# Inverse roots of the latent ranks by a DRAM scratch and one broadcast load instead of two spreads by matmuls

## The reference, cut to what matters

```
def _rms_norm(x, g):
    y = x * lax.rsqrt(jnp.mean(x * x, axis=-1, keepdims=True) + RMS_EPS)
    return y * g

proj = h @ w_in
fq, fk, fv, fg, c_q, c_kv, k_r = jnp.split(proj, cuts, axis=-1)    # c_q: 384 wide, c_kv: 256 wide
fox_out = _fox_attention(fq, fk, fv, log_f)                         # 8 heads of 64
q  = (_rms_norm(c_q,  q_norm)  @ w_uq)                              # 8 heads of 64 + 32
kv = (_rms_norm(c_kv, kv_norm) @ w_ukv)                             # 8 heads of 64 + 64
mla_out = _mla_attention(q_nope, q_rope, k_nope, k_rope, v)
m = concatenate([fox_out, mla_out]) @ w_out
```

## Time and profile before

| | |
|---|---|
| median of 3 runs | 1998.29 us (1997.29 to 1999.68) |
| profiled execution | 1997.75 us |
| its span | 1996.0 us |
| mean granted TensorE clock | 0.998 |
| TensorE busy | 1964.0 us, 98% of the span |
| VectorE busy | 1169.2 us, 59% |
| ScalarE busy | 845.9 us, 42% |
| DMA | 167.66 MB, 84 GB/s |
| start of even_ukv (step 144) | 138.87 us from the start of the span |

### The profile page before, as it was taken

The page is one execution under the profiler, slowest core; times in us unless marked ns, Lnnn a source line. Parts: engine busy times, 40 slices in busy tenths (PEclk is TensorE's granted clock), DMA queues, the critical chain, the costliest instruction groups (busy, mean ns, idle before and its releaser), DMA issues.

```text
span 1996.0 us, 29508 instructions
## 1 busy us (share of the span) xinstructions
PE 1964.0 (98%) x11549; PEld 1616.6 (81%) x11549; DVE 1169.2 (59%) x1939; ACT 845.9 (42%) x1347; POOL 23.6 (1%) x28
## 2 busy tenths in 40 slices
PE   9999999999999999999999999999999899999998
PEld 7776798888888787898888888778778678888887
DVE  6556477534547766567533555877777656424532
ACT  5456544333335455454332333644664633212222
POOL 0111000000000000000000000000000000000000
PEclk9999999999999999999999999999999999999999
DMA  6222122222222111123223224111111122222221
GB/s 215 77 72 96 43 76 95 89 100 106 87 90 98 69 64 64 64 85 106 82 93 115 91 83 138 43 44 45 63 44 44 63 81 89 105 97 94 94 96 64
DMA packets 27583, 167.66 MB, mean 84 GB/s; under 512 B 3272, under 2 KB 3400, under 8 KB 11600
## 3 DMA queue, kind: packets, MB, share of 16 engines
q1 hardware_dynamic: 25872, 161.69, 23.0%
q10 hardware_dynamic: 1600, 4.42, 0.7%
HBM read 162.93 MB, written 2.11 MB: 83 GB/s over the span
## 4 chain that ended last, share of the span: by engine, by line
PE 85%; DVE 7%; ACT 5%; issue 2%; DMA 1%; SPq 0%; DVEq 0%; ACTq 0%
PE bank L506 24%; PE bank L508 24%; PE bank L507 23%; PE bank L1146 2%; PE bank L781 1%; ACT hH L1343 1%; ACT wH L1343 1%; DVE hL L2120 1%; PE bank L970 1%; PE bank L804 1%; PE bank L994 1%; DVE x L2116 1%; PE bank L793 1%; ACT L1343 1%; PE bank L1232 1%
## 5 line engine op out<-in xcount | busy, mean ns | idle before, releaser
L506 PE MATMUL bank<-hH,wH 128*128 128x512 f32 x1368 | 550.0, 402 | 2.0 <-DVE hL L2082 2.0
L508 PE MATMUL bank<-hH,wL 128*128 128x512 f32 x1368 | 532.9, 390 | 0.0
L507 PE MATMUL bank<-hL,wH 128*128 128x512 f32 x1368 | 531.9, 389 | 0.0
L1343 ACT ACTIVATE wH<-raw 128x2048 fp32r<-128x2048 f32 (+3 forms) x199 | 294.1, 1488 | 119.9 <-PE bank L508 105.1
L506 PEld LDWEIGHTS bank<-hH,wH 128*128 128x128 f32 x1368 | 257.4, 188 | 60.0 <-issue 7.1
L508 PEld LDWEIGHTS bank<-hH,wL 128*128 128x128 f32 x1368 | 257.2, 188 | 54.8
L507 PEld LDWEIGHTS bank<-hL,wH 128*128 128x128 f32 x1368 | 257.9, 189 | 46.4
L2031 DVE TENSOR_TENSOR wL<-raw,wH 128x2048 fp32r<-128x2048 f32 x96 | 219.7, 2288 | 125.6 <-ACT wH L1343 125.6
L506 PE MATMUL bank<-mH,wH 128*128 128x512 f32 (+1 forms) x610 | 232.8, 382 | 0.0
L507 PE MATMUL bank<-mL,wH 128*128 128x512 f32 (+1 forms) x610 | 232.6, 381 | 0.0
L508 PE MATMUL bank<-mH,wL 128*128 128x512 f32 (+1 forms) x610 | 232.6, 381 | 0.0
(11 more groups left out here) (344 smaller groups left out, 2864.4 us busy)
## 6 DMA issues: line engine op xcount, KB each, us to landing
raw<-in_ffn_up SPq DMA_DIRECT2D x44, 1024.0 KB, 4.8
raw<-in_mlp_up SPq DMA_DIRECT2D x16, 1024.0 KB, 4.8
raw<-in_mlp_down SPq DMA_DIRECT2D x16, 1024.0 KB, 4.8
raw<-in_ffn_down SPq DMA_DIRECT2D x16, 768.0 KB, 4.3
raw<-in_odd_in SPq DMA_DIRECT2D x12, 1024.0 KB, 4.8
raw<-in_dn_qkv SPq DMA_DIRECT2D x12, 1024.0 KB, 4.8
raw<-in_ffn_down SPq DMA_DIRECT2D x16, 640.0 KB, 3.8
raw<-in_even_in SPq DMA_DIRECT2D x7, 1024.0 KB, 4.9
```

The source lines that it names most:

```text
L506: mm(out, a, c, start=first, stop=False, skip_group_check=joined)
L507: mm(out, a, d, start=False, stop=False, skip_group_check=joined)
L508: return mm(out, b, c, start=False, stop=last, skip_group_check=joined)
L1343: return nc.scalar.activation(out, in_, func, **kw)
```

## The change

The inverses travel through a DRAM scratch of 8 x 128 floats. At step 121 ScalarE stores `stat[:, 48:56]` so that the DRAM holds them in the order of the tokens, c_q first and then c_kv: 128 partitions with 8 values each, written to 8 rows of 128 values. At step 125 ScalarE waits for that store and asks for one load that brings all 1024 values to each of the 128 partitions (`rank_inverse`, 128 x 1024 float32, in a region of SBUF that is free at that time). The two spreads leave TensorE's list. VectorE's scalings read rank_inverse instead of bank 7. The scaling of tiles 0 to 2 moves from step 124 to 132, of tiles 3 and 4 from 127 to 134; the lows from 126 to 134 and from 129 to 136; the highs from 125 to 133 and from 128 to 135.

```diff
+        rank_inverse = sb("rank_inverse", [P, 2, SEQ], F32, qF_at + 4 * 18 * SEQ)
...
                 if t == 116:
                     rank_sums()
-                if t == 123:
-                    pe.wait_ge(*at("cq.inverse"))
-                    spread_tokens(7, 48).then_inc(*tick("spread_pe", "cq.spread"))
-                if t == 127:
-                    pe.wait_ge(*at("cq.t2"))
-                    spread_tokens(7, 52).then_inc(*tick("spread_pe", "ckv.spread"))
...
-                if t in (125, 128):
-                    his("cq", range(3) if t == 125 else (3, 4), cqH, lambda k: cqRaw[:, k, :])
+                if t == 121:
+                    act.wait_ge(*at("cq.inverse"))
+                    act.dma_start(dram["rank_rows"].rearrange("c p -> p c"), stat[:, 48:56], allow_slow_non_contiguous=True)\
+                        .then_inc(*tick("rank_stored", "cq.stored", 16))
+                if t == 125:
+                    act.wait_ge(*at("cq.stored"))
+                    act.dma_start(rank_inverse[:].rearrange("p a n -> p (a n)"),
+                                  dram["rank_rows"].rearrange("c p -> (c p)").unsqueeze(0).to_broadcast([P, 2 * SEQ]))\
+                        .then_inc(*tick("rank_loaded", "cq.spread", 16))
+                if t in (133, 135):
+                    his("cq", range(3) if t == 133 else (3, 4), cqH, lambda k: cqRaw[:, k, :])
...
-                stt(cqRaw[:, k, :], cqRaw[:, k, :], g, bank[7][:], ALU.mult, ALU.mult).then_inc(*tick("norm_dve", f"cq.t{k}"))
+                stt(cqRaw[:, k, :], cqRaw[:, k, :], g, rank_inverse[:, int(k >= 3), :], ALU.mult, ALU.mult).then_inc(*tick("norm_dve", f"cq.t{k}"))
...
-                if t in (124, 127):
-                    dve.wait_ge(*at("cq.spread" if t == 124 else "ckv.spread"))
-                    for k in range(3) if t == 124 else (3, 4):
+                if t in (132, 134):
+                    dve.wait_ge(*at("cq.spread"))
+                    for k in range(3) if t == 132 else (3, 4):
                         rank_scaled(k)
-                if t in (126, 129):
-                    for k in range(3) if t == 126 else (3, 4):
+                if t in (134, 136):
+                    for k in range(3) if t == 134 else (3, 4):
                         lo_tile("cq", k, cqRaw[:, k, :], cqH, cqL)
...
+        dram["rank_rows"] = nc.dram_tensor("rank_rows", (8, P), F32, kind="Internal").ap()
```

## The result

The changed kernel takes 2003.9 us (median of 9 runs, 2003.09 to 2006.11) against 1998.72 us of the kernel before in the same session: ratio 1.0027, 95% interval 1.0018 to 1.0035. It is slower by more than the 0.2% that can be told from no change. The profiled execution has a span of 2002.1 us, 6.1 more than before. The forecast was 1996.5, range 1994.9 to 2001.0, with 0.13 for slower.

What follows compares the result with a forecast made beforehand. TensorE was taken to bound the kernel: 0 for the unchanged arithmetic, minus 1.78 us for the spreads, 0 for a hidden store and load, so minus 1.8 from the median 1998.29 gives 1996.5 us, range 1994.9 to 2001.0.

Steps and rivals of the forecast that it cites:

- What bounds the kernel, and what the removal is worth: TensorE, busy 98% of the span, bounds; removing two spreads of 0.89 us each from its path gives minus 1.78 us.
- S: Latency of ScalarE's store of the inverses to DRAM, taken as 4.0 us; up to 4.8 us costs TensorE nothing.
- the upper bound of 13.2: Store latency in us at 183 ns for each of 64 packets on an engine, read from the stored 2 KB rows.
- my lower bound: Store latency of 2.0 us: 64 packets per engine at 8.5 ns each, from the program's first load.
- The rival for "slower": Each 4-byte write takes its own DRAM time, from 142 ns a packet; TensorE stands at step 144; 2004.9 us; chance 0.12.
- The estimate of 2.7 us: Store latency by the skill page's figures: about 10.5 ns a packet and some 2.0 us fixed; the sum unchanged.
- The floor of 1.49 us: Least store latency: gate rows' store issued at 38.97, its waiting load at 40.46, so 1.49 us at most.
- The store's issue: ScalarE's store at step 121 goes out at 118.4, after its earlier work ends at 118.37.
- The three deadlines for the store: Landing by 123.2 for TensorE's step 144; by 124.0 for tile 11's turn and for the values at 127.9, called looser.
- the formula max(0, S - 4.8): TensorE's stall ahead of step 144: store latency beyond the 4.8 us from issue at 118.4 to deadline 123.2.
- The clock: A clock fall behind TensorE's wait at step 144 would add more; the trace's fall, 4 us at 0.57, lost 1.7 us.
- my chance of a third for missing it: Two rivals with TensorE waiting at step 144: part of the gain comes back, chance 0.22; slow store, chance 0.12.

Runs made afterwards that it cites:

- the turned store: Changed kernel plus one transposing matmul on TensorE and a ScalarE copy, so the store writes eight runs of 512 bytes: median 1997.07 us against 1999.05, ratio 0.9987.
- the one row: Changed kernel storing only one of the eight columns, 128 runs of 4 bytes side by side in 512 bytes; load reads the gate's rows: 1999.77 us, single run.

## Why the prediction was wrong

**What bounds the kernel, and what the removal is worth: right.** Minus 1.78 us was the term; the store of 32-byte runs gives 1.76, with nothing else changed. The wait for the rotated queries moved along (1.21 us at 170.74 in the changed kernel, 1.31 before). A stage shorter by the 1.8 us of the sum is what the changed kernel shows with a quick store.

**How long is S: the step that failed.** I took 4.0 us, and 12.44 was measured, near the upper bound of 13.2. That it stayed under the bound was luck: the bound was 183 ns a packet on the DMA engine, and the packets passed at 9 ns each, my lower bound, all of them in 0.8 us. I chose 4.0 by the wrong likeness: a 4-byte write was set beside a 32-byte read because of its size. The time lies behind the packets, and it depends on where the writes go: it is there when they are close neighbours in the DRAM (12.44 us) and gone when they are 64 bytes apart (4.94). The rival for "slower" came nearest, with a chance of 0.12: it named the neighbours in a 512-byte row. But it put the price on each 4-byte write, from 142 ns a packet on; 512 writes cost nearly as much as 1024, and 1024 writes that lie apart cost next to nothing. That the neighbours come from different partitions, as the rival had it, is neither shown nor refuted. Why close writes delay each other no run shows.

The Trainium skill ("DMA: Bandwidth & Descriptors", "Specifications") says that below 512 bytes the DMA reads, changes and writes back. The runs fit a stretch of 512 bytes and don't exclude 256. They add the price, some 45 ns for each further write into 512 bytes, and that small writes apart from each other have next to none. The estimate of 2.7 us from that page's figures was further off than mine, and its 2.0 us fixed is the page's figure for DMAs that GpSimd issues, not for ScalarE's.

**The floor of 1.49 us: right for a quiet DMA, not here.** The store of the gate rows was made with the DMA engines idle (its 16 packets are all that the earlier trace rows has). Here some 3 us pass behind the weights of unit 10, which SyncE had asked for 0.57 us earlier:

```profile
115.98 0.33 SPq L439 DMA_DIRECT2D raw<-in_even_uq  x1
```

I never put the two side by side, though SyncE's request stands in the trace of the kernel before.

**The store's issue: 118.4 in the text, 116.55 in the trace.** ScalarE's queue handed the DMA out while its exponentials still ran (they end at 117.6). That gave 1.1 us more room beyond the 0.73 by which this execution was ahead, and was not enough.

**Which deadline: mixed.** The three deadlines for the store were 123.2 for step 144 and 124.0 twice. With the store landed at 128.97 both kinds are missed by 5 to 6 us, as the load on SyncE's queue shows from the other side. But TensorE stops at the first it reaches, the turn of tile 11, and that stop moves step 144 back far enough that no wait is left there. I called those deadlines looser and forecast the stop at step 144; 0.8 us of difference said nothing about which would be seen. So the formula max(0, S - 4.8) is right only by luck: with 12.44 for S it gives a stall of 7.6 and 2004.1 us, beside 2003.9 measured. The stop was shorter (5.25 us, with the store issued earlier) and at another place, and the lower clock, which the formula has not, added 2.66.

**The clock: in the right direction, and too small.** The rival for "slower" said that a fall behind such a wait would add more, and read 1.7 us for one from the earlier trace rows; here the stretch from the turn to step 144 is 2.66 us longer.

## What to carry to other kernels

A scatter of small values into the DRAM is dear for the close neighbours its writes have, within 512 bytes or perhaps 256, far more than for its number of runs or its bytes; one small transposition on chip that makes the rows contiguous cost 0.1 us of TensorE here and brought the load's issue forward by 8. When a transfer replaces engine work, bound its latency by a row of the same direction, add what the queues carry at that moment, and look for the first instruction behind the wait that TensorE needs, not for the last. Where the bounds lie as far apart as 2.0 and 13.2 us and the slack is 4.8, my chance of a third for missing it had no row behind it.

## What the runs showed of the hardware

- The end of a store can be signalled long after its packets: 8.7 us after the last recorded packet for 1024 writes of 4 bytes into eight rows of 512 bytes.
- The slower such a store, the later, by and large, lands a load that is under way: 768 KB of weights landed 4.0 us after their issue in the kernel before, 4.1 beside the turned store, 7.2 beside the eight rows and 9.8 beside the one row.
- A stop of TensorE of 5.2 us was followed by 6.6 us at a granted clock of 0.58, the stop of 7.41 us by 6.6 us at 0.53, the one of 4.36 us by 6.6 us at 0.57. Behind the stop of 2.30 us of the one row the clock stayed at 1.00. The stretches behind 7.41 and 2.30 us:

```profile
144.40:151.00 6.60, 6.55 (x15) 0.53 0.43 110
```
```profile
128.40:134.00 5.60, 5.55 (x30) 1.00 0.18 64
```

- VectorE's reciprocal takes 3.35 us for 128 x 512 float32 values, against 0.69 us for a product of that size.
